# MLP up products as seven half products in place of eight in a decoder trunk on one Trainium2 core

## The reference

```
def rmsnorm(x, g):
    return x * rsqrt(mean(x * x, -1) + EPS) * g
def sq_relu_mlp(x, w_up, w_down):
    h = relu(x @ w_up)
    return (h * h) @ w_down
# per layer: x = x + mixer(rmsnorm(x, norm_mix)); x = x + sq_relu_mlp(rmsnorm(x, norm_ffn), w_up, w_down)
# at the end: rmsnorm(x, final_norm)
```

## Time and profile before

| what | us |
|---|---|
| median of 3 runs (2458.06 to 2462.01) | 2461.59 |
| the profiled execution | 2460.99 |
| its span, first to last instruction | 2459.2 |
| PE busy in it | 2388.9 |
| DVE busy | 1173.2 |
| ACT busy | 662.0 |
| POOL busy | 165.1 |

### The profile page before, as it was taken

How to read it: one execution, slowest core, us unless ns; L and a number is a source line. 1 busy time by engine, 2 the same in 40 slices (tenths; PEclk the granted TensorE clock), 3 DMA queues, 4 the chain that set the end, 5 groups by cost and what they waited for, 6 DMA issues and landing times.

```text
span 2459.2 us, 37030 instructions
## 1 busy us (share of the span) xinstructions
PE 2388.9 (97%) x15530; PEld 2284.5 (93%) x15530; DVE 1173.2 (48%) x2067; ACT 662.0 (27%) x1130; POOL 165.1 (7%) x222
## 2 busy tenths in 40 slices
PE   6999999989999999999999999999999999999999
PEld 6889898878999999999999877869999999999998
DVE  5545555568434334334336665476534334334343
ACT  3232222234212112112113354253312112112124
POOL 3000000013000000000002011012000000000003
PEclk8999999999999999999999999999999999999999
DMA  3212121101111111111112311101111111111111
GB/s 107 52 36 66 48 66 38 45 27 44 44 52 44 44 52 43 44 52 43 43 52 63 91 31 50 35 10 43 43 52 44 44 52 43 44 52 44 43 61 71
DMA packets 177416, 120.55 MB, mean 49 GB/s; under 512 B 23623, under 2 KB 173044, under 8 KB 177220
## 3 DMA queue, kind: packets, MB, share of 16 engines
q1 hardware_dynamic: 177108, 118.10, 16.4%
q10 hardware_dynamic: 144, 0.02, 0.0%
HBM read 110.94 MB, written 12.33 MB: 50 GB/s over the span
## 4 chain that ended last, share of the span: by engine, by line
PE 74%; issue 20%; DVE 3%; POOL 2%; ACT 1%; SPq 0%; POOLq 0%; DMA 0%; ACTq 0%; DVEq 0%
PE acc L1704 57%; PE acc L2032 3%; PE acc L2034 3%; PE acc L2033 3%; PE acc L2051 2%; PE acc L2074 1%; PE acc L2062 1%; POOL small L1034 1%; PE acc L1972 1%; PE acc L1973 1%; PE acc L1974 1%; DVE x_res L1289 0%; DVE w_lo L1085 0%; DVE q_t L1553 0%; DVE prob L1587 0%
## 5 line engine op out<-in xcount | busy, mean ns | idle before, releaser
L1704 PE MATMUL acc<-x_hi,w_hi 128*128 128x352 f32 x1560 | 506.1, 324 | 10.4 <-DVE x_lo L1091 6.7
L1704 PE MATMUL acc<-x_lo,w_hi 128*128 128x352 f32 x1560 | 500.8, 321 | 0.0
L1704 PE MATMUL acc<-x_hi,w_lo 128*128 128x352 f32 x1560 | 500.7, 321 | 0.0
L1704 PE MATMUL acc<-h_hi,w_hi 128*128 128x352 f32 x1440 | 464.6, 323 | 0.0
L1704 PE MATMUL acc<-h_lo,w_hi 128*128 128x352 f32 x1440 | 461.4, 320 | 0.0
L1704 PE MATMUL acc<-h_hi,w_lo 128*128 128x352 f32 x1440 | 461.0, 320 | 0.0
L697 ACT ACTIVATE w_hi<-w_raw 128x1024 fp32r<-128x1024 f32 x176 | 185.2, 1053 | 610.3 <-PE acc L1704 522.7
L1163 DVE TENSOR_TENSOR x_res<-x_res,acc 128x1056 f32<-128x1056 f32 x120 | 150.4, 1254 | 372.6 <-PE acc L1704 372.6
L1704 PEld LDWEIGHTS acc<-x_hi,w_hi 128*128 128x128 f32 x1560 | 293.4, 188 | 12.4 <-issue 12.4
L1704 PEld LDWEIGHTS acc<-x_lo,w_hi 128*128 128x128 f32 x1560 | 293.8, 188 | 0.7 <-issue 0.7
L1704 PEld LDWEIGHTS acc<-x_hi,w_lo 128*128 128x128 f32 x1560 | 293.4, 188 | 0.0
(11 more groups left out here) (280 smaller groups left out, 3269.4 us busy)
## 6 DMA issues: line engine op xcount, KB each, us to landing
w_raw<-in_w_up SPq DMA_DIRECT2D x64, 512.0 KB
w_raw<-in_w_down SPq DMA_DIRECT2D x64, 512.0 KB
w_raw<-in_w_mlstm_in SPq DMA_DIRECT2D x24, 512.0 KB
x_in<-in_x_prompt SPq DMA_DIRECT2D x8, 512.0 KB, 4.1
w_raw<-in_w_mlstm_out SPq DMA_DIRECT2D x8, 512.0 KB
w_raw<-in_w_q SPq DMA_DIRECT2D x16, 256.0 KB
w_raw<-in_w_attn_out SPq DMA_DIRECT2D x16, 256.0 KB
out_y_prompt<-y_out SPq DMA_DIRECT2D x8, 512.0 KB, 2.6
```

What stands on the lines that cost most here:

```text
L1704: last = T.matmul(out[:, b], w[:, k, m], x[:, TN * b:TN * b + TN], start=(k == 0 and i == 0), stop=(k == k_chunks - 1 and i == 2))
```

## The change

The up product of a block of now 256 inner units (2 x 128) over 1024 channels (even and odd chunks of 128) and 1056 tokens (two halves of 528) is a 2 x 2 by 2 x 2 block product. It is made as seven half products in place of eight, by Strassen's scheme in Winograd's form: S1 to S4 are sums of weight quarters (POOL, `weight_sum`), T1 to T4 sums of quarters of the input (POOL, `item_sum`, made once a layer), and the seven products are combined by seven additions (U2, U3, U4, C11, C12, C21, C22; DVE, `combine`; the first product is copied out by ACT, `keep_first`). A half product is 4 chunks x 2 x 3 matmuls of 264 columns.

For this the gains of the norm go into the up weights (DVE, `with_gain`, in w_raw) and the input operands are x_res itself, split in quarters (`item_high`, `item_low`, tables `ROW_ITEMS` and `ROW_SUMS`). The tokens' norm is put in after the product: POOL multiplies z by the reciprocal of the mean square (`scale`), DVE multiplies that by max(z, 0) (`square_of_relu`), and ACT and DVE split the result. No square root is taken for it.

There are 16 blocks a layer. A `down` has still 8 rows of x_res, each now of 2 chunks x 9 = 18 matmuls of 352 columns, so there are twice as many additions to x_res. `down(f)` follows `up(f + 1)`, and h of block f + 1 is made in the queues of `down(f)`, with the gains, half sums and first splits of block f + 2. Weights are split in halves and quarters of a slab. `mlp_mean_square` comes at the end of `up(0)`. The last `down` takes the first token part in two passes, one for each of the last two blocks. The diff, cut to the parts of the steady loop and the tables:

```diff
+HN = TOK // 2
+QN = HN // 2
+FIRST_H, SECOND_H = slice(0, HN), slice(HN, TOK)
+FILLS = (0, 1, 3, 2, 4, 5, 6)
+POS = {j: i + 1 for i, j in enumerate(FILLS)}
+UP_SLOT = (2, 3, 0, 1, 2, 3, 0)
+DOWN_SLOT = (1, 2, 3, 0)
+LAYER_FILLS, LAYER_ROWS = 11 * NF, 8 * NF
+GROUP = {0: 0, 4: 0, 1: 4, 2: 2, 5: 2, 3: 6, 6: 6}
+STEPS_OF = {"U2": 1, "U3": 2, "C11": 3, "U4": 4, "C22": 5, "C21": 6, "C12": 7}
...
+ROW_ITEMS = {0: [], 1: [("B11", 0), ("T1", 0)], 2: [("T2", 0), ("T3", 0)], 3: [("B11", 1), ("T1", 1), ("T4", 0)],
+             4: [("T2", 1), ("T3", 1)], 5: [("B11", 2), ("T1", 2), ("T4", 1)], 6: [("B11", 3), ("T2", 2), ("T3", 2)],
+             7: [("T1", 3), ("T2", 3), ("T3", 3), ("T4", 2)]}
+REST_ITEMS = [("B21", j) for j in range(4)] + [("T4", 3)] + [("B22", j) for j in range(4)]
+ITEMS = [x for r in range(8) for x in ROW_ITEMS[r]] + REST_ITEMS
+ITEM_AT = {x: i + 1 for i, x in enumerate(ITEMS)}
+ROW_SUMS = {0: [("T1", 0)], 1: [("T3", 0), ("T2", 0)], 2: [("T1", 1)], 3: [("T3", 1), ("T2", 1), ("T4", 0)], 4: [("T1", 2)],
+            5: [("T3", 2), ("T2", 2), ("T4", 1)], 6: [("T1", 3)], 7: [("T3", 3), ("T2", 3), ("T4", 2), ("T4", 3)]}
+SUMS = [x for r in range(8) for x in ROW_SUMS[r]]
+SUM_AT = {x: i + 1 for i, x in enumerate(SUMS)}
...
 def walk_mlp(eng, layer, up, down, last=None):
+    s = (S_MLP0, S_MLP1)[layer]
+    up(At(0), At(s))
+    up(At(1), At(s + 2))
+    down(At(0), At(s + 4))
+    n = (NF - 4) // 2
+    with eng.Fori(0, n) as i:
+        up(At(2, i, 2), At(s + 6, i, 8))
+        down(At(1, i, 2), At(s + 8, i, 8))
+        up(At(3, i, 2), At(s + 10, i, 8))
+        down(At(2, i, 2), At(s + 12, i, 8))
+    s += 8 * n + 6
+    up(At(NF - 2), At(s))
+    down(At(NF - 3), At(s + 2))
+    up(At(NF - 1), At(s + 4))
+    if last is not None:
+        last(At(s + 6))
+    else:
+        down(At(NF - 2), At(s + 6))
+        down(At(NF - 1), At(s + 8))
...
+            def weight_sum(layer, f, s, j):
+                b = f + NF * layer
+                a1, a2 = raw(s + 1, 8), raw(s, 8)
+                even, odd = slice(0, 8, 2), slice(1, 8, 2)
+                if j == 1:
+                    pool.wait_ge(g_ready, (b.times(2) + 1).value)
+                    if not (layer == 0 and static(f, 0)):
+                        done = At(LAYER_FILLS) if static(f, 0) else up_fills(layer, At(0)) + 7 if static(f, 1) else up_fills(layer, f + -1) + 7
+                        pool.wait_ge(op_lo, done.value)
+                    x = nc.gpsimd.tensor_tensor(s_tmp[:], a2[:, even], a2[:, odd], ALU.add)
+                if j == 3:
+                    pool.wait_ge(g_ready, (b.times(2) + 2).value)
+                    pool.wait_ge(ss_ready, (b.times(4) + 1).value)
+                    x = nc.gpsimd.tensor_tensor(a2[:, even], a1[:, even], a2[:, even], ALU.subtract)
+                if j == 2:
+                    pool.wait_ge(op_lo, (up_fills(layer, f) + POS[1]).value)
+                    x = nc.gpsimd.tensor_tensor(s_tmp[:], s_tmp[:], a1[:, even], ALU.subtract)
+                if j == 6:
+                    pool.wait_ge(op_lo, (up_fills(layer, f) + POS[2]).value)
+                    x = nc.gpsimd.tensor_tensor(s_tmp[:], a1[:, odd], s_tmp[:], ALU.subtract)
+                x.then_inc(ss_ready, 1)
+            def scale(layer, f, c):
+                b = f + NF * layer
+                pool.wait_ge(z_dve, (b.times(7) + (7 - c)).value)
+                nc.gpsimd.tensor_tensor(h_scaled[:, f.parity, c], z_of(f)[c], rstd[:], ALU.mult).then_inc(tz_ready, 1)
...
+            def mlp(layer):
+                def up(f, s):
+                    weight_sum(layer, f, s, 6)
+                    if static(f, 0):
+                        for k in range(4, KD):
+                            sum_chunk(2 * layer, k)
+                        for j in (1, 3, 2):
+                            weight_sum(layer, f + 1, s + 2, j)
+                    if static(f, 1):
+                        pool.wait_ge(ms_ready, 2 + 2 * layer)
+                        scale(layer, At(0), 1)
+                        scale(layer, At(0), 0)
+                def down(f, s):
+                    if not static(f, NF - 1):
+                        scale(layer, f + 1, 1)
+                        scale(layer, f + 1, 0)
+                    if not (static(f, NF - 1) or static(f, NF - 2)):
+                        for j in (1, 3, 2):
+                            weight_sum(layer, f + 2, s + 2, j)
...
+            def combine(layer, f, name):
+                b = f + NF * layer
+                z1, z2 = z_of(f)
+                c11, c12, c21, c22 = (blocks(z[:, v], 2) for z in (z1, z2) for v in (FIRST_H, SECOND_H))
+                out, kept, j, earlier = {"U2": (c22, c12, 2, None), "U3": (c21, c22, 3, "U2"), "C11": (c11, c12, 4, None),
+                                         "U4": (c12, c22, 1, "C11"), "C22": (c22, c21, 1, "U4"), "C21": (c21, c21, 5, "C22"),
+                                         "C12": (c12, c12, 6, "U4")}[name]
+                if name == "U2":
+                    dve.wait_ge(z_act, (b + 1).value)
+                if earlier is not None:
+                    dve.wait_ge(z_dve, (b.times(7) + STEPS_OF[earlier]).value)
+                dve.wait_ge(up_done, (b.times(7) + (j + 1)).value)
+                V.tensor_tensor(out, kept, halves(layer, j), ALU.add).then_inc(z_dve, 1)
+            def square_of_relu(layer, f, c):
+                dve.wait_ge(tz_ready, ((f + NF * layer).times(2) + (2 - c)).value)
+                z = z_of(f)[c]
+                V.scalar_tensor_tensor(z, z, 0.0, h_scaled[:, f.parity, c], ALU.max, ALU.mult).then_inc(zz_ready, 1)
+            def h_low(layer, f, c):
+                dve.wait_ge(hh_ready, ((f + NF * layer).times(2) + (2 - c)).value)
+                V.tensor_tensor(h_lo[:, f.parity, c], z_of(f)[c], h_hi[:, f.parity, c].bitcast(F32), ALU.subtract
+                                ).then_inc(hl_ready, 1)
+            def add_row(layer, f, k):
+                dve.wait_ge(row_done, (f.times(8) + (LAYER_ROWS * layer + k + 1)).value)
+                V.tensor_tensor(blocks(x_res[:, k]), blocks(x_res[:, k]), row_banks(layer, k), ALU.add).then_inc(row_taken, 1)
...
+            def with_gain(layer, s):
+                norm = (FFN0, FFN1)[layer]
+                dve.wait_ge(w_loaded[s.parity], landed(s).value)
+                V.tensor_tensor(raw(s, 8), raw(s, 8), gains[:, norm * KD:norm * KD + KD].unsqueeze(2).to_broadcast([P, KD, P]),
+                                ALU.mult).then_inc(g_ready, 1)
+            def entry_row(layer, r):
+                for name, j in ROW_ITEMS[r]:
+                    item_low(layer, name, j)
+                at = ((0, 3), (3, 5))[layer]
+                if r in at:
+                    with_gain(layer, At((S_MLP0, S_MLP1)[layer] + at.index(r)))
...
+                    if not static(f, 0):
+                        combine(layer, f, "U2")
+                    combine(layer, f, "U3")
...
+                        down_low(layer, f + -1, s + 2, 0)
+                        for name in ("C11", "U4", "C22"):
+                            combine(layer, f, name)
+                        down_low(layer, f + -1, s + 2, 1)
+                        if static(f, 1):
+                            square_of_relu(layer, At(0), 1)
+                            square_of_relu(layer, At(0), 0)
+                            h_low(layer, At(0), 1)
+                            h_low(layer, At(0), 0)
+                        combine(layer, f, "C21")
+                        down_low(layer, f + -1, s + 2, 2)
+                        combine(layer, f, "C12")
+                        down_low(layer, f + -1, s + 2, 3)
...
+                def down(f, s):
+                    for k in range(KD):
+                        if not static(f, NF - 1):
+                            if k < 2:
+                                square_of_relu(layer, f + 1, 1 - k)
+                            if k in (1, 2):
+                                h_low(layer, f + 1, 2 - k)
+                        if static(f, NF - 1) and k == 7:
+                            split(At(S_KV))
+                        add_row(layer, f, k)
+                        if static(f, NF - 1):
+                            dve.wait_ge(row_taken, LAYER_ROWS * layer + 8 * (NF - 1) + k + 1)
+                            mark(x_final)
+                            prepare(2, KV, k)
+                        elif static(f, NF - 2):
+                            if k % 2 == 1:
+                                down_low(layer, f + 1, s + 2, k // 2)
                         else:
+                            if k in (0, 2):
+                                with_gain(layer, s + (2 + k // 2))
+                            if k == 3:
+                                up_low(layer, f + 2, s + 2, 0)
+                            if k == 5:
+                                up_low(layer, f + 2, s + 2, 1)
+                                up_low(layer, f + 2, s + 2, 3)
...
+                def product(f, j, before):
```

(72 more changed lines are left out.)

694 lines of the change are left out of this document (438 added, 256 removed).

## The result

The changed kernel takes 2621.22 us (median of 4 runs, 2620.58 to 2625.56) against 2459.82 us for the kernel before (4 runs, 2456.18 to 2462.01): 1.0661 times as long, 95% interval 1.0642 to 1.068. The forecast was 2545, with a range up to 2590. The direction was right and the size was not: 76 us are missing from the sum.

The account below looks back on a forecast made before the run. TensorE, 97% busy, was taken as the bound, with DVE and POOL keeping ahead. From 2461.0 us: -69.4 + 89.6 + 0.9 + 41 + 10.6 + 5 + 7 = +84.7, say 2545; range 2430 to 2590.

Parts of the forecast that it names:

- What bounds the kernel: Whole span: TensorE 97% busy; fewer columns shorten it directly, only while DVE and POOL keep ahead of PE.
- The price of a 264-column matmul: Up products: 123.3 ns per matmul, bounds 122.2 and 133.3, giving -69.4 us over 32 blocks.
- Added on DVE and POOL, the exclusion: MLP blocks: DVE 27 us per 43.6 us block, POOL 10; two-SBUF DVE operations and POOL hold each other up.
- One steady block, walked: Each steady down: PE's row 3 starts 3.2 us late, waiting for row 1's addition; 28 x 3.2 = +89.6 us.
- Starts of the layers: Entries and blocks 0 and 1: DVE/POOL collisions and the reciprocal cost +41 us, 27 in layer 0, 14 in layer 1.
- Ends: Layer 0's last down: add, mark, x_hi, x_lo chain of 4.18 us a row, +10.6 us; last down's second-half h, +5.
- Turns of the loop: Loop runs 12 times in place of 6, one turn having left TensorE 1.2 us without issue: +7 us.
- Collisions don't cost: Rival, between C12 and row 1's addition: POOL and DVE run side by side, stalls 11 us, total 2446; chance 0.22.
- Starts only: Rival, steady downs: queue order falls kindly, row 3 in time, but entries cost as forecast; 2467; chance 0.14.
- the narrow matmul: Rival, up products: 264 columns no cheaper than 288, 133.3 ns each, 54 us more, 2599; chance 0.08.

## Why the prediction was wrong, step by step

- *What bounds the kernel.* Right: fewer columns shorten the span only as long as DVE and POOL keep ahead, and they didn't.
- *The price of a 264-column matmul.* Taken 123.3 ns, is 120.8, below the lower bound of 122.2; worth 13 us. By the Trainium skill (TensorE: Matmul & The Clock Gate, Back-to-back issue gap), 112.5 ns, the 83 us that the prediction gave for it happen to be the measured 82; but the page, which gives that formula for an isolated matmul, has both widths too short, 149.2 for 158.9 and 112.5 for 120.8, and only their difference agrees.
- *Added on DVE and POOL, the exclusion.* Right, and shown: squares of 3.52 us beside the scale, additions and combinations not held, the whole wait gone once POOL's operations are narrow or on DVE.
- *One steady block, walked.* The walk was right in the main (row 3 forecast 3.2 us late; 2.6 there and 0.3 one row ahead; the block 46.8, and 46.87 where the clock stays). **The step that failed is its price**, 28 x 3.2 = +89.6: the wait was counted as idle time alone. In 23 of 26 periods TensorE comes out of it at the 1.2 GHz level and loses another 1.71 us, in three of these 3.41. The term measured +141 us. That is 51 of the 80 us missing in the profiled execution; the starts below miss 48, and the matmul's price and the turns, 13 and 7 too high, take 20 back. The Trainium skill (TensorE: Matmul & The Clock Gate, HAM oscillation — how this bites in real kernels) describes this pattern, a wait in every turn of a loop from which the array restarts at the lower clock each time. The page's waits are for a DMA and longer, about 3 to 5 us; here 2.9 us in two pieces were enough in 23 of 26 periods. The runs with 18 matmuls in the wait and with the gains later agree that the wait brings it about. The prediction had used that page only for the spacing.
- *Starts of the layers.* The second step that failed by its size: 41 forecast, 22 + 27 in layer 0, and 14 and some 26 in layer 1, about 90 in all. The mechanisms are there (chunk sums, reciprocal), but the collisions are larger: the eight additions ahead of MLP 0 take 47.4 us, not 38, and in block 0 PE waits three times (5.56, 3.18 and 3.47 us) where 7 us were counted. And here too the waits were priced as idle time alone, while 12 and 14 us of the two stretches from entry to first down are matmuls at the lower clock. For layer 1 it was wrong that the slower additions leave POOL the time: the eight additions ahead of MLP 1 take 53.4 us for 43.8, so 10 of the 14 arise where nothing was counted. How the collisions part between the chunk sums and the rest was measured only for the former, 27 us.
- *Ends.* Right in sum, 12 for 11.5 in layer 0, and some 5 for 5 in the tail; in layer 0 partly by luck. The chain is 3.84 us a row and not 4.18, so six rows cost 0.98 each, and one row costs 4.3 because a weight split that collides with POOL's sum (3.43 us) stands in it. With the chain gone half of the 10 us remains.
- *Turns of the loop.* Wrong by 7: no turn shows in a period of 43.35.
- *The rivals.* "Collisions don't cost" and "Starts only" fell with the first timeline; the narrow matmul was cheaper, not dearer.

## What to carry over

A wait that recurs in front of TensorE must be priced twice: the idle time, and what the granted clock loses afterwards. Here 2.9 us of idle cost 4.6 in most blocks while 0.3 us cost nothing extra, so making such a wait short, by order alone, gave back 105 us. An idle engine isn't a free place for work when it shares a lock with a busy one: a scale moved from idle POOL (7% busy before) to DVE (64%) cost 1.25 us where it had cost 2.9 plus 2.3 of DVE. And a scheme that saves an eighth of TensorE's columns in one stage pays only once every one of its sums is off the path, which took moving every sum of the MLPs from POOL and three changes of order on DVE, for a gain of 0.8%.
